# Inverse softmax sums of an encoder's attention: spread over 64 columns by VectorE and turned by one transpose, in place of two products

## What is computed

```python
def attend(q_blk):
    s = jnp.einsum('bkgqd,bksd->bkgqs', q_blk, kh) * scale
    p = jax.nn.softmax(s, axis=-1)
    return jnp.einsum('bkgqs,bksd->bkgqd', p, vh)
o = lax.map(attend, qb)
```

## Time and profile before

| | |
|---|---|
| time, median of 3 runs | 1642.25 us |
| the three runs | 1640.09, 1642.25, 1642.68 us |
| span of the profiled execution | 1637.3 us |
| PE busy in the span | 1564.5 us (96%) |
| DVE busy | 620.3 us (38%) |
| ACT busy | 432.4 us (26%) |
| POOL busy | 377.4 us (23%) |
| granted TensorE clock, mean | 0.999 |

### The profile page before, as it was taken

How to read it: one execution, slowest core, us unless ns; L and a number is a source line. 1 busy time by engine, 2 the same in 40 slices (tenths; PEclk the granted TensorE clock), 3 DMA queues, 4 the chain that set the end, 5 groups by cost and what they waited for, 6 DMA issues and landing times.

```text
span 1637.3 us, 20617 instructions
## 1 busy us (share of the span) xinstructions
PE 1564.5 (96%) x8370; PEld 818.0 (50%) x8370; DVE 620.3 (38%) x1222; ACT 432.4 (26%) x782; POOL 377.4 (23%) x440
## 2 busy tenths in 40 slices
PE   8999999989999999998999999999999999999986
PEld 5645666456444444443357546655554444444432
DVE  1787635462122112311328966274521222123114
ACT  3554641211111111111235647302111111111102
POOL 5572870000000000000364538500000000000003
PEclk9999999999999999999999999999999999999999
DMA  9300303669999999999940013056699999999996
GB/s 394 128 1 14 142 1 78 257 265 410 427 426 427 426 428 426 427 427 428 362 183 1 1 36 120 1 160 271 272 411 418 427 426 428 426 428 426 429 428 270
DMA packets 54946, 468.77 MB, mean 286 GB/s; under 512 B 19081, under 2 KB 19209, under 8 KB 28322
## 3 DMA queue, kind: packets, MB, share of 16 engines
q1 hardware_dynamic: 47602, 451.12, 66.5%
q0 software_dynamic: 7104, 16.24, 2.7%
q10 hardware_dynamic: 144, 0.07, 0.0%
HBM read 446.44 MB, written 26.74 MB: 289 GB/s over the span
## 4 chain that ended last, share of the span: by engine, by line
PE 77%; DMA 14%; DVE 5%; ACT 2%; issue 1%; POOL 1%; SPq 0%; POOLq 0%; ACTq 0%; DVEq 0%
PE bank L929 21%; DMA ring<-wu 14%; PE bank L587 11%; PE bank L959 10%; PE bank L921 7%; PE bank L723 7%; PE bank L662 2%; PE bank L581 2%; PE bank L649 2%; PE bank L677 2%; PE bank L946 1%; PE bank L558 1%; PE bank L893 1%; PE bank L905 1%; PE bank L777 1%
## 5 line engine op out<-in xcount | busy, mean ns | idle before, releaser
L930 PE MATMUL bank<-ring,hbuf 128*64 128x512 f32 x704 | 309.7, 593 | 0.0
L2112 POOL DMA_INDIRECT expert_rows<-raw_qd,store_rows x60 | 58.7, 979 | 1046.9 <-ACT raw_qd L1329 883.5
L929 PE MATMUL bank<-ring,hbuf 128*64 128x512 f32 x640 | 281.2, 593 | 14.6 <-DMA ring<-wu 14.0
L1864 DVE COPY raw_qd<-bank 128x256 f32<-128x256 f32 x64 | 27.2, 425 | 668.6 <-PE bank L946 668.6
L587 PE MATMUL bank<-hbuf,ring 128*128 128x512 f32 x480 | 210.0, 594 | 0.0
L929 PEld LDWEIGHTS bank<-ring,hbuf 128*64 128x64 f32 x640 | 86.5, 137 | 191.6 <-issue 191.6
L929 PE MATMUL bank<-raw_qd,hbuf 128*64 128x512 f32 x372 | 163.7, 592 | 7.3 <-DMA hbuf<-wu 4.9
L959 PE MATMUL bank<-ring,raw_qd 128*64 128x512 f32 x352 | 160.5, 598 | 5.2 <-DVE raw_qd L1864 5.2
L961 PE MATMUL bank<-ring,raw_qd 128*64 128x512 f32 x352 | 160.5, 598 | 0.0
L921 PE MATMUL bank<-raw_qd,x 128*128 128x192 f32 x896 | 159.5, 332 | 0.0
L1322 ACT ACTIVATE raw_qd<-bank 64x512 f32<-64x512 f32 x64 | 37.8, 591 | 431.3 <-PE bank L930 431.3
(11 more groups left out here) (387 smaller groups left out, 2263.9 us busy)
## 6 DMA issues: line engine op xcount, KB each, us to landing
ring<-wu SPq DMA_DIRECT2D x44, 2048.0 KB, 22.9
ring<-wd SPq DMA_DIRECT2D x44, 2048.0 KB, 22.5
ring<-wg SPq DMA_DIRECT2D x40, 2048.0 KB, 21.1
ninth_slot<-wd SPq DMA_DIRECT2D x20, 2048.0 KB, 22.5
hbuf<-wu SPq DMA_DIRECT2D x20, 2048.0 KB, 22.4
raw_qd<-wg SPq DMA_DIRECT2D x18, 2048.0 KB, 19.5
ring<-w_in SPq DMA_DIRECT2D x8, 2048.0 KB, 15.6
raw_qd<-wg SPq DMA_DIRECT2D x6, 1792.0 KB, 11.4
```

The source lines that it names most:

```text
L929: mm(pb[2 + par][0:CAP, :], tokens[:, k, :], gates[k], start=(k == 0), stop=(k == KT - 1))
L930: last = mm(pb[2 + par][CAP:P, :], tokens[:, k, :], ups[:, k, :], start=(k == 0), stop=(k == KT - 1))
L2112: G.indirect_dma_start(out=half_rows, out_offset=bass.IndirectOffsetOnAxis(ap=store_i[:, e:e + 1], axis=0), in_=y_sb[e % 2], in_offset=Non ...
```

## The change

VectorE's reciprocal reads `p_sum` with each head's column repeated 64 times and writes 128 x 128 inverse sums (`p_inv` moves from a 2-column corner of `small` to 128 free columns of the ring for each of its two buffers). TensorE no longer makes the two products; one 128 x 128 transpose turns the inverse sums, behind the eight value products, and the wait for `pn` moves there with it. `pv` is now signalled by the transpose.

```diff
-        p_sum, p_bias, p_inv = ([small[:, 4 * k + 2 * i:4 * k + 2 * i + 2] for i in range(2)] for k in range(3))
+        p_sum, p_bias = ([small[:, 4 * k + 2 * i:4 * k + 2 * i + 2] for i in range(2)] for k in range(2))
+        p_inv = [ring[:, 1, 3840 + P * i:3968 + P * i] for i in range(2)]
...
             def values(u):
-                pe.wait_ge(s["pn"], on("pn") + u + 1)
                 if u >= 2:
                     pe.wait_ge(s["o_b"], on("o_b") + u - 1)
                 bank = A_BANK[u % 2]
-                for i in range(2):
-                    mm(bank[HD * i:HD * i + HD, P:2 * P], p_inv[u % 2][:, i:i + 1].broadcast_to([P, HD]), ident,
-                       start=True, stop=True)
                 pe.wait_ge(s["pt_e"], on("pt_e") + u + 1)
                 for j in range(NB):
                     for i in range(2):
                         r = slice(HD * i, HD * i + HD)
-                        last = mm(bank[r, 0:P], av[:, j, r], pT_sb[u % 2][:, i, P * j:P * j + P],
-                                  start=(j == 0), stop=(j == NB - 1))
-                last.then_inc(s["pv"], 1)
+                        mm(bank[r, 0:P], av[:, j, r], pT_sb[u % 2][:, i, P * j:P * j + P],
+                           start=(j == 0), stop=(j == NB - 1))
+                pe.wait_ge(s["pn"], on("pn") + u + 1)
+                tr(bank[:, P:2 * P], p_inv[u % 2], ident).then_inc(s["pv"], 1)
...
-                V.reciprocal(p_inv[u % 2], p_sum[u % 2]).then_inc(s["pn"], 1)
+                V.reciprocal(p_inv[u % 2].rearrange("p (h c) -> p h c", h=2),
+                             p_sum[u % 2][:, :, None].broadcast_to([P, 2, HD])).then_inc(s["pn"], 1)
```

## The result

| | before | changed |
|---|---|---|
| median of the runs taken together | 1641.67 us (4 runs) | 1650.13 us (4 runs) |
| lowest and highest | 1640.09 to 1642.68 | 1644.93 to 1653.73 |
| span of the profiled execution | 1637.3 us | 1643.0 us |
| ratio, 95% interval | | 1.0046, 1.0031 to 1.0060 |

The changed kernel is slower by 8.5 us (0.46%), where 1644.3 us and no measurable change were forecast; the median lies outside the range of 1640.4 to 1647.4. The profiled execution took 1644.93 us in all, at a mean granted clock of 0.999.

What follows compares the result with a forecast made beforehand. PE was taken as the bound (busy 96% of the span), with ACT's copy bounding middle units once the products go. Second layer +0.77 and first +1.24 made +2.0 us: 1642.25 + 2.0 = 1644.3, range 1640.4 to 1647.4.

Steps and rivals of the forecast that it cites:

- The saved products and the transpose: Attention on PE: removed products save 0.10 per middle unit, lone transpose adds 0.11 in every unit; second layer +0.77 us.
- the copy's term: Middle units: with the products gone, ACT's copy sets the value products' start, 2.21 us behind the transposes instead of 2.35.
- The rival that the saving is real: Middle units: ACT's copy does not hold PE, so 0.15 us saved in each; total 1641.0; chance 0.13.
- bounds L677: it starts 2.21 behind the transposes: Middle units: value products L677 wait for ACT's copy, giving 2.21 + 1.02 + 0.11 = 3.34 us a unit.
- The second rival: Lone transpose costs 0.20 us instead of 0.11; 30 units on the path add 2.7: 1647.0; chance 0.13.
- the prediction's own sign (3.4 or more): Middle units in the changed profile: a period of 3.4 us or more would prove the second rival; 3.34 was forecast.
- The reciprocal: On DVE, 128 x 128 takes 0.96 us, 0.80 more; fits in the unit, with DVE's idle time about 0.6.
- the rival that POOL holds it: Each new reciprocal waits for POOL's running instruction, 0.6 to 1.0 us in some 22 units: 1655 to 1664; chance 0.05.
- a reciprocal above 1.5 us: Rival: a dearer reciprocal makes DVE bound the units; at 2 us, +12 us in all; chance 0.03.
- The hold in the first layer: L1559, long behind POOL, makes DVE late; reciprocal's 0.80 us passes to PE, 0.16 returns; first layer +1.24.
- not enough to fall behind it: Second layer: DVE gets about 0.15 us later, so L1559 still starts before POOL's first large multiplication.
- theory A: Of the repeat experiments: clock drop belongs to the change; a 12.07 us output projection in about every second changed-kernel profile.

Runs made afterwards that it cites:

- the hoisted kernel: Changed kernel with PE's wait for `o_b` moved ahead of the unit's scores: 1645.03 us, 1.0023; on another chip 1646.58, 1.0028.
- those of the second: Second group: the changed kernel again, unedited, five rounds beside the kernel before: 1648.45 us against 1641.57, 1.0037.
- the filled kernel's repeat: Changed kernel, `o_b` wait ahead of scores, two unused products before the last three units' `pt_e` wait: 1643.47 us, 1.0014; repeated on another chip 1649.99, 1.0033.

## Why the prediction was wrong

The decomposition comes from stages, one part taken away at a time, in us for a layer:

| | stage | step |
|---|---|---|
| changed | 59.33 | |
| the `o_b` wait ahead of the scores | 58.69 | 0.64 |
| products between the last waits | 58.41 | 0.28 |
| `head_norm` early, no hold | 57.13 | 1.28 |
| before, with `head_norm` early | 56.37 | 0.76 |

The steps depend somewhat on their order, since slack of one unit hides in the hold of another; the sum does not. It is 2.96 a layer. Of twice that, the kernel before pays 0.61 as well: 5.3 us net.

**The saved products and the transpose: right in sum, in part by luck.** A layer was to cost 0.77, and costs 0.76 once nothing else disturbs it. L671 did fill a gap in which PE would otherwise wait for ACT, so their removal saves next to nothing; the lone transpose lies within its bounds. (It takes 0.16 to the next transposes, but these, with one of their own shape in front of them, are through 0.05 sooner, 1.04 against 1.09 in the earlier trace rows, and products start 2.15 behind instead of 2.21. So 2.15 + 1.03 + 0.16 makes the 3.34 that 2.21 + 1.02 + 0.11 were to make: the transpose was put 0.05 too low and the copy's term 0.06 too high, and the two cancel. In the layer's sum too, 0.17 for the first unit and 0.20 for the end stand where 0.11 and 0.26 were forecast.) The rival that the saving is real (1641.0 or less) falls: in no kernel is a middle unit at 3.17.

**The copy "bounds L677: it starts 2.21 behind the transposes": this step failed.** The 2.21 was read off last units of the kernel before. There L671 stands between the wait for `o_b` and the wait for `pt_e`. The change takes it away, and the two waits come to stand in a row in front of the value products. The row was right, but for other surroundings than those it was carried to. In the new surroundings 2.24 is measured. That looks like only 0.03 too much, but the same transposes with the waits taken apart give 2.15, and transposes of 1.09 give 2.21 behind one wait and 2.30 behind two in a row. So a period is 3.43 instead of 3.34, and the last units are hit alike. Taking the waits apart, by scores or by products of no use, brings 3.34 back. It makes 0.92 a layer, 1.84 in all: some ten of the 14 units that wait for `o_b` pay their 0.09, those ahead of the hold vanish in it. The second rival, the dear lone transpose, has the right period and by the prediction's own sign (3.4 or more) would be proven, but it has the wrong place: PE spends the time ahead of the value products, where the chain's "issue" grows from 0.04 to 0.14. What PE's sequencer does in the 0.09 no view shows.

**The reciprocal: right.** It takes 0.94 where 0.96 was forecast, and DVE's idle time before `row_max` is 0.47, with 0.27 ahead of the copy, where 0.6 was. All 32 last 941 to 952 ns while POOL works, so the rival that POOL holds it falls, and with it the one of a reciprocal above 1.5 us. The Trainium skill's repeat count of 8 (VectorE: DVE Perf Modes, § First, the fixed hardware budget), from which 1.2 us was estimated, doesn't agree with the 0.94 measured. Its other rule, that VectorE contends with GpSimd in instructions of two SBUF inputs (SBUF — State Buffer, § Who interferes with whom), agrees: L1557 with two such inputs is held for 4.25, the reciprocal with one never is.

**The hold in the first layer: right in mechanism, somewhat low.** It was to cost 0.80 − 0.16 and to swallow 0.17 of the units ahead of it, so 1.24 − 0.77 = 0.47 more than a layer without it. It costs 1.28 against 0.61, 0.67 more. The long reciprocal alone, without the transpose, costs 0.74 there.

**The second layer's hold, "not enough to fall behind it": wrong, and worth 1.28.** The prediction weighed by how much DVE would be late. DVE is in fact not later: its L1557 starts 10.15 behind the third scores (995.88 against 985.73), against 10.27 before. It is POOL that starts earlier, 9.91 behind them against 11.11. The reason lies in SP's queue, ahead of attention's middle. SP writes the diagonal layer's input `u` to DRAM, and its next issue, the reads of it, waits for that write; behind them comes the table load that POOL waits for (`s5p`). SP's timeline before:

```profile
974.36 0.81 SPq L435 DMA_DIRECT2D u_scratch<-raw_qd  x2
978.54 3.75 SPq L439 DMA_DIRECT2D raw_qd<-u_scratch  x8
```

and of the changed kernel:

```profile
977.08 0.81 SPq L436 DMA_DIRECT2D u_scratch<-raw_qd  x2
979.77 4.38 SPq L440 DMA_DIRECT2D raw_qd<-u_scratch  x8
```

Before, 4.2 us pass between the two issues, in the changed kernel 2.7. The queues' table for half a microsecond, first of the kernel before (976.0 to 976.5, inside its write), then of the changed one (982.0 to 982.5, long behind it); columns are packets, MB, and the share of 16 engines:

```profile
q8 instruction: 1, 0.02, 11.7%
```

```profile
q8 instruction: 1, 0.02, 12.3%
```

In the kernel before a fetch of instructions falls into the write. In the changed kernel it comes when the write has landed. The 18 profiles divide alike, and in the first layer, where no fetch falls into the write, all have 2.7. The kernels with PE's 8370 records of before (the four of before, the long reciprocal alone, the early norms, the products behind) have 4.2 to 4.8 us between the issues, and DVE is held in the second layer of none. Those with fewer (8274 to 8306) have 2.7, and DVE is held, except where `head_norm` is early, and once in the hoisted kernel. There POOL started 11.05 behind the third scores in spite of the 2.7, so the gap is not all that sets its start. That the change, by shortening PE's program, moves the fetch and so frees POOL early fits the profiles but that one; it was not tried by itself, for instance by idle instructions elsewhere in PE's stream, and is argued, not shown. What is shown is that the hold in the second layer comes with the transpose's half of the change, not with the long reciprocal, and that early `head_norm` removes it.

**The sum.** 2.0 was forecast, 1.5 for the transposes and 0.5 for the first layer's hold; these two measure 1.5 and 0.7. Missing are 1.84 for the waits and 1.28 for the second layer's hold: 5.3 in all. The first group's medians stand 8.5 apart, those of the second 6.9, the means of four spans each (1644.6 and 1638.9) 5.7. The rest above 5.3 is not located. One candidate is PE's clock behind attention. Here is the kernel with the transpose and the short reciprocal, in windows over the end of the first layer's attention (length, busy times of PE, PEld, DVE, ACT and POOL, then the granted clock):

```profile
225.00:230.00 5.00, 2.85 (x31) 2.22 (x29) 1.03 (x5) 1.94 (x2) 4.84 (x3) 1.00 0.00 0
230.00:233.00 3.00, 1.99 (x18) 1.31 (x19) 0.58 (x2) 0.11 (x1) 3.00 (x1) 0.95 0.00 0
233.00:236.00 3.00, 3.00 (x5) 1.33 (x4) 0.00 (x0) 0.00 (x0) 2.94 (x3) 0.50 0.00 0
```

PE, busy for 2.85 of 5 us before it, is granted 0.50, the 1.2 GHz level, from 233.00 to 236.00, just behind the start of the output projection (232.36), and the projection takes 12.1 us instead of 10.4: 1.7 lost. This occurs in 4 of 16 stages of the kernels that leave the last gap empty, in 1 of 2 of the one with two transposes in it, and in 1 of 18 of those with products in it (the filled kernel's repeat). In the changed kernel itself it is 1 of 8, before 0 of 8. Two further profiles of the changed kernel, in which theory A expected it about every second time, do not show it. That is too few to say that it belongs to the change, and it stays open.

**A version that beats both** was not found. The kernel before with early `head_norm` has the shortest stages, 0.61 less in the first layer, and 0.9994 (0.9984 to 1.0003) can't be told from it. With every loss but the transpose taken away, the changed kernel is at 1.0004 (0.9993 to 1.0014), and its stages are still 0.76 a layer longer: the idea itself gains nothing here, since the products that it replaces cost next to nothing.

## What to carry to other kernels

A duration read between two events belongs to everything that stands between them in the engine's stream. Before carrying it to a changed stream, write out both streams with their waits; here a wait moved next to another one, and 0.09 us went some ten times a layer. An instruction that starts a microsecond ahead of what would hold it is not safe because one's own edit leaves it in time: check what sets the start of the other side, down to its transfers. And work that stands in a gap costs next to nothing, so replacing it by cheaper work mostly shows what the new arrangement costs elsewhere.

## What the hardware showed that I had not expected

- Two semaphore waits in a row ahead of a product, the second of which ends late: 0.14 us from release to product, against 0.04 behind one wait or where other work of PE stands between the two.
- A reciprocal of 128 columns whose input is two columns repeated 64 times takes 0.94 us, which is 6.2 ns for each column beyond the 155 ns of two. The 32 columns of the earlier trace rows, which are not repeated, come to 6.4, so repeating the input adds nothing that shows.
- 4.2 to 4.8 us between a write to DRAM of two transfers and the issue that waits for it in the 7 profiles in which a fetch of instructions falls into the write (second layer), and 2.7 in the 11 in which it doesn't. That the fetch is the cause was not tried by itself.
- Behind waits of 4.90 and 3.50 us inside attention PE's granted clock fell to 0.60 and 0.50. Behind the 1.07 of the changed kernel it stayed at 1.00.
